# A third weight buffer for the experts of a transformer block, with x2 kept in memory meanwhile

## What is computed

```python
p_group = softmax(t @ w_rg + b_rg)          # 4 groups, the best one is taken
p_exp   = softmax(logits of its 4 experts)  # the best two are taken
y = sum over the two: weight * (silu(t @ w_gate[e]) * (t @ w_up[e])) @ w_down[e]
x = x2 + g2 * y
return rms_norm(x, final_norm)
```

## Time and profile before

| | us |
|---|---|
| median of 3 runs | 833.36 (833.19 to 833.53) |
| the profiled execution, whole | 836.89 |
| its span in the profile | 835.2 |
| routing ends, first gather issued | 507.03 |
| PE's last down product ends | about 800.5 |

### The profile page before, as it was taken

One profiled execution on the slowest core, in us unless ns is written; L12 is line 12 of the kernel. 1 busy time (PEld: TensorE's weight loads), 2 busy tenths in 40 slices (PEclk: granted clock), 3 DMA queues, 4 the chain that ended last, 5 costly groups with the idle time before them and its releaser, 6 DMA issues.

```text
span 835.2 us, 8861 instructions
## 1 busy us (share of the span) xinstructions
PE 702.7 (84%) x3377; PEld 397.4 (48%) x3377; DVE 335.3 (40%) x743; ACT 177.6 (21%) x427; POOL 131.2 (16%) x171
## 2 busy tenths in 40 slices
PE   0469899999999998889999815999998999899920
PEld 0455445667675796555544513444443344334300
DVE  4932566866575434867221174011211111021107
ACT  3203225121121213557121201111211112011103
POOL 8650022313050281000000001000000000000021
PEclk9669999999999998989999855999999999999975
DMA  9899802222220305510520422489999999999935
GB/s 335 262 312 276 288 0 101 101 102 101 101 101 1 53 1 192 191 73 2 202 94 19 168 97 64 165 281 401 374 388 396 381 399 383 399 369 397 398 110 230
DMA packets 88092, 173.49 MB, mean 208 GB/s; under 512 B 19347, under 2 KB 23533, under 8 KB 88045
## 3 DMA queue, kind: packets, MB, share of 16 engines
q1 hardware_dynamic: 78048, 151.12, 50.8%
q0 software_dynamic: 4240, 15.21, 5.6%
q10 hardware_dynamic: 5756, 6.52, 2.3%
HBM read 157.63 MB, written 15.20 MB: 207 GB/s over the span
## 4 chain that ended last, share of the span: by engine, by line
PE 66%; DVE 14%; DMA 12%; ACT 3%; issue 2%; POOL 1%; SPq 0%; ACTq 0%; POOLq 0%; DVEq 0%
PE ps L962 14%; DMA gu<-in_w_up 10%; PE ps L1067 7%; PE ps L2107 6%; PE ps L2074 5%; PE ps L955 3%; PE ps L989 3%; DVE acc L1733 3%; PE ps L2185 2%; PE ps L2191 2%; PE ps L2071 2%; PE ps L983 2%; PE ps L2098 2%; PE ps L2195 2%; PE ps L636 1%
## 5 line engine op out<-in xcount | busy, mean ns | idle before, releaser
L962 PE MATMUL ps<-gu,xgT 128*128 128x512 f32 x256 | 117.0, 617 | 8.3 <-DMA gu<-in_w_up 5.9
L962 PEld LDWEIGHTS ps<-gu,xgT 128*128 128x128 f32 x256 | 49.9, 198 | 70.5 <-issue 63.7
L1401 POOL DMA_INDIRECT xg<-xn_rows,list x16 | 15.0, 940 | 413.1 <-PE ps L943 221.2
L2107 PE MATMUL ps<-hT,winr 128*128 128x512 f32 x144 | 72.1, 609 | 0.0
L1733 DVE SCALAR_TENSOR_TENSOR acc<-ada,st,acc 128x512 f32<-128x512 f32 x84 | 68.1, 811 | 2.3
L1067 PE MATMUL ps<-wout,yT 128*128 128x512 f32 x128 | 58.6, 617 | 0.0
L955 PE MATMUL ps<-gu,xgT 128*64 128x512 f32 x256 | 56.7, 595 | 0.0
L989 PE MATMUL ps<-dn,hidT 128*128 128x512 f32 x128 | 56.5, 594 | 0.0
L1038 DVE TENSOR_TENSOR hidm<-sg,ps 128x512 f32<-128x512 f32 x8 | 5.5, 686 | 121.6 <-ACT sg L1005 121.6
L1587 POOL TENSOR_TENSOR cc<-low,lev 128x512 f32<-128x512 f32 x20 | 30.2, 1520 | 129.7 <-DVE low L1919 104.2
L2074 PE MATMUL ps<-hT,wind 128*128 128x512 f32 x96 | 42.3, 593 | 0.0
(11 more groups left out here) (401 smaller groups left out, 1041.9 us busy)
## 6 DMA issues: line engine op xcount, KB each, us to landing
gu<-in_w_gate SPq DMA_DIRECT2D x16, 2048.0 KB, 14.6
gu<-in_w_up SPq DMA_DIRECT2D x16, 2048.0 KB, 20.5
dn<-in_w_down SPq DMA_DIRECT2D x16, 2048.0 KB, 20.5
ada<-in_w_ada SPq DMA_DIRECT2D x12, 2048.0 KB, 10.4
expert_rows<-zero POOLq DMA_DIRECT2D x9, 512.0 KB, 10.8
expert_rows<-yo ACTq DMA_DIRECT2D x8, 512.0 KB, 6.7
wout<-in_w_out SPq DMA_DIRECT2D x1, 3072.0 KB, 10.7
x<-in_x SPq DMA_DIRECT2D x2, 1024.0 KB, 6.2
```

What stands on the lines that cost most here:

```text
L962: ins = nc.tensor.matmul(PS[2 * b + w][:, :], T["xgT"][:, k, :], gu[b][:, w, k, :], start=(k == 0), stop=(k == KT - 1))
L2107: ins = t.matmul(bank[:, :], w(k), T["hT"][:, k, :], start=(k == 0), stop=(k == KT - 1))
```

## The change

- A third buffer: `gu2` (32 KB a partition, from `RX`) and `dn2` (16 KB, in x2's place). Tile n uses buffer n % 3. SP issues gate/up n when gate/up n-3 is done and down n-1 when down n-4 is done.
- Experts 0, 1 and 2 are pinned. The order becomes B B B s B s B s B s B s B s s s; the tile sizes are the same, eight of 128 rows and eight of 64.
- x2 goes to memory in four stores behind the last `xn2` store, and comes back as `x3` (in the second down buffer's place) when down 13 is done. The final sum works on `x3`. `fnb` is loaded just before, after gate/up 14.
- Gate/up and down weights of expert 2 are loaded after the x2 stores are issued and after their room is free.
- g2 is copied out of `g2b` by ACT (`g2m`, `g2s`, and an unused `g2q`), before the routing's exponentials; DVE's two copies go.
- Routing: one link more in the tile starts, one operation more for the padded rank; `EXTRA` is 10. Several semaphores become one with counts (`routing`), set at the same places.

```diff
     at("x2", R1 + 64 * K + 256, [P, ST, D])
+    at("dn2", R1 + 64 * K + 256, [P, FT, D])
+    at("x3", RW + 16 * K, [P, ST, D])
...
+    at("gu2", RX, [P, 2, KT, F])
...
-    ORDER = [0, 1]
-    for m in range(BIG - 2):
-        ORDER += [BIG + m, 2 + m]
-    ORDER += [E - 2, E - 1]
+    ORDER = list(range(NBUF))
+    big, less = list(range(NBUF, BIG)), list(range(BIG, E))
+    rest = less[::-1] if NBUF == 3 else less
+    while big:
+        ORDER.append(rest.pop(0))
+        ORDER.append(big.pop(0))
+    ORDER += rest[::-1] if NBUF == 3 else rest
...
-        sp.dma_start(T["fnb"][:], A["final_norm"].partition_broadcast(P)).then_inc(sem("fn_in"), 16)
-        sp.wait_ge(sem("experts"), 1)
+        for i in range(ST):
+            sp.dma_start(x2_d[i * P:(i + 1) * P, :], T["x2"][:, i, :]).then_inc(sem("x2_st"), 16)
+        sp.wait_ge(sem("g2_moved"), 1)
+        sp.wait_ge(sem("ss"), 2 * ST)
+        sp.wait_ge(sem("logit_mm"), ST)
+        for b in range(2):
+            sp.wait_ge(sem(f"xn2_st{b}"), 32)
+        load_gate_up(sp, 2, 2)
+        sp.wait_ge(sem("x2_st"), 16 * ST)
+        load_down(sp, 2, 2)
+        sp.wait_ge(sem("routing"), ROUTING["experts"])
         expert = {}
-        for n in range(2, E + 1):
+        for n in range(NBUF, E + 1):
...
-                sp.wait_ge(sem("gu_mm"), n - 1)
-                load_gate_up(sp, expert[n], n % 2)
-            if n >= 3:
-                sp.wait_ge(sem("dn_mm"), n - 2)
-                load_down(sp, expert[n - 1], (n - 1) % 2)
+                sp.wait_ge(sem("gu_mm"), n - NBUF + 1)
+                load_gate_up(sp, expert[n], n % NBUF)
+            if n > NBUF:
+                sp.wait_ge(sem("dn_mm"), n - NBUF)
+                load_down(sp, expert[n - 1], (n - 1) % NBUF)
+
+        sp.wait_ge(sem("gu_mm"), E - 1)
+        sp.dma_start(T["fnb"][:], A["final_norm"].partition_broadcast(P)).then_inc(sem("fn_in"), 16)
+        sp.wait_ge(sem("dn_mm"), E - 2)
+        sp.dma_start(T["x3"][:], x2_d.rearrange("(i p) d -> p i d", p=P)).then_inc(sem("x3_in"), 16)
...
+        act.wait_ge(sem("oproj_mm"), ST)
+        act.wait_ge(sem("ada_out"), HPS - 4)
+        for name, m in (("g2m", P), ("g2s", 64), ("g2q", 32)):
+            d = D * m // P
+            for s in range(P // m):
+                ins = a.activation(T[name][m * s:m * s + m, :], T["g2b"][m * s:m * s + m, s * d:(s + 1) * d], ACT.Copy)
+        ins.then_inc(sem("g2_moved"), 1)
         act.wait_ge(sem("exp_in"), 1)
...
-        link(v.scalar_tensor_tensor(e16[:], rank, float(HALF), pad.unsqueeze(1).broadcast_to([P, ST, E]), ALU.is_ge,
-                                    ALU.mult))
+        wide_pad = pad.unsqueeze(1).broadcast_to([P, ST, E])
+        link(v.tensor_tensor(e16[:], rank, wide_pad, ALU.add))
+        link(v.scalar_tensor_tensor(e16[:], e16[:], float(P), wide_pad, ALU.is_ge, ALU.mult))
...
-        for e in range(2):
-            link(g.memset(T["pinned"][:, e:e + 1], (2 - e) * 1e6))
+        for e in range(NBUF):
+            link(g.memset(T["pinned"][:, e:e + 1], (NBUF - e) * 1e5))
```

More of the change, by code:

```diff
@@ L48 @@
 FT = F // P
[L49 to L53, removed]
+EXTRA = 10
+NBUF = 3
+ROUTING = {"chosen": 1, "places": 2, "slots": 3, "list": 4, "experts": 5, "w12": 6, "route_i": 7}
+ROUTING_PE = {"rank_mm": 1, "list_mm": 2}
+SIZES = [128] * 8 + [64] * 8
+TILE_START = [sum(SIZES[:n]) for n in range(E + 1)]
+TILE_START += [TILE_START[E] + P * (n + 1) for n in range(EXTRA - 1)]
 ROWS = TILE_START[-1] + P
+BIG = SIZES.count(P)
+STEPS_DOWN = [n for n in range(1, E) if SIZES[n] < SIZES[n - 1]]
 EPS = 1e-6
@@ L854, in build, with rows_of @@
     wd_v = A["w_down"][0].rearrange("g e (k p) d -> (g e) p k d", p=P)
-    gu, dn = (T["gu0"], T["gu1"]), (T["dn0"], T["dn1"])
-    ORDER = [0, 1]
-    for m in range(BIG - 2):
-        ORDER += [BIG + m, 2 + m]
-    ORDER += [E - 2, E - 1]
+    gu, dn = [T[f"gu{b}"] for b in range(NBUF)], [T[f"dn{b}"] for b in range(NBUF)]
+    ORDER = list(range(NBUF))
[5 more added lines that the diff above has]
+    ORDER += rest[::-1] if NBUF == 3 else rest
+    def rows_of(n):
+        return SIZES[ORDER[n]] if n < E else P
     def small(n):
-        return n < E and ORDER[n] >= BIG
-    NB = E // 2
+        return rows_of(n) < P
     STORED = [1]
     for n in range(E + EXTRA):
-        STORED.append(STORED[-1] + (2 if small(n) else 1))
+        STORED.append(STORED[-1] + P // rows_of(n))
     def load_gate_up(q, e, b):
@@ L940, in pe_rows @@
             pe.wait_ge(sem("xgT_d"), n)
-        m = HALF if small(n) else P
+        m = rows_of(n)
         for k in range(KT):
@@ L945, in pe_rows, with buffer_of, loads_of, pe_gate_up @@
         ins.then_inc(sem("xg_tr"), 1)
-    def pe_gate_up(pe, n, b, came):
-        pe.wait_ge(sem(f"gu_in{b}"), came)
+    def buffer_of(n):
+        return n % NBUF if n < E else 0
+    def loads_of(n):
+        if n < E:
+            return n // NBUF + 1
+        return len(range(0, E, NBUF)) + n - E + 1
+    def pe_gate_up(pe, n, b):
+        w_in = gu[buffer_of(n)]
+        pe.wait_ge(sem(f"gu_in{buffer_of(n)}"), 32 * loads_of(n))
         pe.wait_ge(sem("xgT_a"), n + 1)
         pe.wait_ge(sem("xgT_d"), n + 1)
+        m = rows_of(n)
         if small(n):
+            parts = P // m
+            f = F // parts
             for k in range(KT):
-                for s in range(2):
+                for s in range(parts):
                     ins = nc.tensor.matmul(
-                        PS[2 * b][HALF * s:HALF * s + HALF, :].rearrange("p (w f) -> p w f", w=2),
-                        T["xgT"][:, k, 0:HALF], gu[b][:, :, k, s * GW:(s + 1) * GW], start=(k == 0),
-                        stop=(k == KT - 1))
+                        PS[2 * b][m * s:m * s + m, 0:2 * f].rearrange("p (w f) -> p w f", w=2),
+                        T["xgT"][:, k, 0:m], w_in[:, :, k, s * f:(s + 1) * f], start=(k == 0), stop=(k == KT - 1))
         else:
@@ L968, in pe_hidden, with pe_down @@
         pe.wait_ge(sem("hidm"), n + 1)
-        for f in range(2 if small(n) else FT):
+        for f in range(FT * rows_of(n) // P):
             ins = nc.tensor.transpose(PS[2 * b][:, f * P:(f + 1) * P], T["hidm"][:, f * P:(f + 1) * P], idf[:])
         ins.then_inc(sem("hid_tr"), 1)
-    def pe_down(pe, n, b, came):
+    def pe_down(pe, n):
+        w_in = dn[buffer_of(n)]
         pe.wait_ge(sem("hidT"), n + 1)
-        pe.wait_ge(sem(f"dn_in{b}"), came)
+        pe.wait_ge(sem(f"dn_in{buffer_of(n)}"), 16 * loads_of(n))
         pe.wait_ge(sem("yo_d"), n + 1)
+        m = rows_of(n)
         if small(n):
+            parts = P // m
+            per = FT // parts
+            d = D // parts
             for f in range(FT):
[L981 to L985, removed]
+                s, c = f // per, f % per
+                for w in range(parts):
+                    ins = nc.tensor.matmul(PS[4][m * w:m * w + m, 0:d], T["hidT"][:, c, m * s:m * s + m],
+                                           w_in[:, f, w * d:(w + 1) * d], start=(f == 0), stop=(f == FT - 1))
         else:
@@ L1016, in act_output @@
         start = TILE_START[ORDER[n] if n < E else n]
[L1017 to L1023, removed]
+        m = rows_of(n)
+        d = D * m // P
+        for s in range(P // m):
+            act.dma_start(yo_d[start:start + m, s * d:(s + 1) * d], T["yo"][m * s:m * s + m, 0:d]
+                          ).then_inc(sem("yo_st"), 16)
     def dve_rows(dve, n):
         dve.wait_ge(sem("xg_tr"), n + 1)
-        m = HALF if small(n) else P
+        m = rows_of(n)
         for k in range(4, KT):
@@ L1128, in pe_moe @@
                            start=False, stop=(i == ST))
-        ins.then_inc(sem("rank_mm"), 1)
-        pe.wait_ge(sem("places"), 1)
+        ins.then_inc(sem("routing_pe"), 1)
+        pe.wait_ge(sem("routing"), ROUTING["places"])
         for n in range(2):
@@ L1282, in dve_moe @@
         link(v.tensor_reduce(order, versus, AX.X, ALU.add))
-        link(v.tensor_scalar(t16, order, -float(BIG), 0.0, ALU.add, ALU.max))
         link(v.tensor_scalar(tile0, order, float(P), None, ALU.mult))
-        v.scalar_tensor_tensor(tile0, t16, -float(P - HALF), tile0, ALU.mult, ALU.add)
-        link(v.tensor_scalar(pad, order, BIG - 0.5, float(P - HALF), ALU.is_gt, ALU.mult))
+        for m, n in enumerate(STEPS_DOWN):
+            less = float(SIZES[n - 1] - SIZES[n])
+            link(v.tensor_scalar(t16, order, -float(n), 0.0, ALU.add, ALU.max))
+            link(v.scalar_tensor_tensor(tile0, t16, -less, tile0, ALU.mult, ALU.add))
+            if m:
+                link(v.tensor_scalar(t16, order, n - 0.5, less, ALU.is_gt, ALU.mult))
+                link(v.tensor_tensor(pad, pad, t16, ALU.add))
+            else:
+                link(v.tensor_scalar(pad, order, n - 0.5, less, ALU.is_gt, ALU.mult))
         link(v.tensor_tensor(cnt, cnt, pad, ALU.add))
@@ L1321, in dve_moe @@
                                       T["tok"][:, i:i + 1], ALU.is_equal, ALU.mult)
[L1322 to L1325, removed]
```

(12 more changed lines are left out.)

69 lines of the change are left out of this document (37 added, 32 removed).

## The result

The changed kernel takes **825.07 us** (median of 5 runs, 824.21 to 829.30); the kernel before takes 833.36. The ratio is 0.9891, 95% interval 0.9862 to 0.9920: 1.1% faster; the medians differ by 8.3 us. The profiled execution took 829.30 with a span of 827.6, 7.6 us less than the span before.

A forecast was written before the change was run, and what follows sets the result against it. The prediction took the experts' stage to be bound by DMA at the margin, through short lead as much as rate. Terms -10.37 + 0.37 + 0.26 = -9.7 us took 833.36 to 823.7 us, range 821.5 to 829.

The forecast's parts named there:

- Starvation of 10.37 us goes: Experts' stage: PE's waits for gate/up weights and the slower products behind them vanish, 10.37 us gained.
- The early load in the idle stretch, done by 505: Before the experts: expert 2's weights load while DMA idles, ending about 505, ahead of the first gather at 507.03.
- The term of 0: First gather: collision with the early load was worth 0 to 2.1 us, and 0 was taken.
- the second rival: First gathers: the early load collides and gather 0 lands 2.1 us late, at most some 4; 825.8 to 828, chance 0.12.
- The lead of 41.8 us against 31 to 34: Big tiles' gate/up loads: a third buffer gives 41.8 us of lead instead of 19.9; landing needs 31 to 34 at worst.
- At the end, 28 us for a load of 10.6 with a backlog of about 10: Three last small tiles: gate/up 15 has 28 us before PE wants it, for a 10.6 us load plus backlog.
- PE should not wait at all: Experts' stage: PE never waits for weights, and its clock stays at 1.00 from the second product on.
- The added steps: DVE's routing chain gains 0.37 us, POOL's tenth empty `If` 0.26; ACT's g2 copies and x3's return cost nothing.
- Rival 1: Experts' stage: DMA's own pace stays the bound, PE waits some 5 us near the end; 828 to 829, chance 0.12.
- The rule: Experts' stage: at the skill's 358 GB/s an estimated 9 us would come back, giving about 832.8; the trace's 397 disagreed.

The follow-up runs named there:

- e3: The changed kernel with x2 stored four times instead of once, so expert 2's early loads run across the first gathers: 827.84 us, ratio 0.9919.
- e1: The changed kernel with expert 2's weights asked for only when gate/up 0 is done, so nothing streams during the routing: 834.01 us, ratio 0.9989.
- e9: The changed kernel with 2 MB copied memory to memory on SP's queue ahead of the load of gate/up 12: 831.62 us, ratio 0.9942.
- e6: The changed kernel with the four least chosen experts in tiles of 32 rows instead of 64, room for 12 extra tiles: 824.53 us, ratio 0.9864.
- e2: The changed kernel with gate/up n issued only when n-2 is done and down n-1 when n-3 is done, early load kept: 842.94 us, ratio 1.0098.
- e7: The changed kernel with 32-row tiles for four experts, hidden 15 copied ahead of store 14, and output 15 in its own tile: 822.14 us, ratio 0.9844.
- e5: The changed kernel with the old rank operation, no link in the tile starts and `EXTRA` = 9: 826.64 us, ratio 0.9886.
- r1: The changed kernel unaltered, run again in a second set of runs: 826.12 us against 836.90 before the change, ratio 0.9887.

## Why the prediction was right

The forecast was 823.7 us, the result 825.07. Its terms:

- *Starvation of 10.37 us goes.* Measured on the stage: 10.40. The step from the pairs' starts to this term was exact, the wait for gate/up is gone in all profiles of the change, and the clock with it: from the second on the big products take 13.7 to 14.0 us, none 15.71.
- *The early load in the idle stretch, done by 505.* It lay in the idle stretch, but its last part landed at 507.8, 3 us later than forecast. No wait of SP's did that, since DMA was at a share of 1.00 or more from 476 to 505; this profile's issues began 0.9 us later than those of the earlier trace rows, the last 15 us went at 391 GB/s instead of 397, and the rest isn't separated. The first gather, issued 1.6 us later than before, missed it by 0.8 us and landed in 4.58 us. The term of 0 was right with less margin than the sum gave. e3 shows the second rival with its forecast price of 2 to 4 us.
- *The lead of 41.8 us against 31 to 34.* Right where it was worked out: gate/up 9 ended at 687.47 (the big product of 695.58 follows it by 8.1 us), and the big product that needed the load began at 729.25. The load landed at 718.8, after 31.3 us; the forecast was 31 to 34.
- *At the end, 28 us for a load of 10.6 with a backlog of about 10.* This is the mis-sized term, and that PE didn't wait here is partly luck. By that sum 7.4 us were to spare; 1.7 us were. The second halves of the last four gate/up loads in the change, from SP's issues, the landing times and PE's chain (us):

| gate/up | issued | to landing | landed | product begins | spare |
|---|---|---|---|---|---|
| 12 | 690.81 | 28.0 | 718.8 | 729.25 | 10.4 |
| 13 | 711.08 | 26.7 | 737.8 | 747.80 | 10.0 |
| 14 | 730.24 | 25.2 | 755.4 | 762.74 | 7.3 |
| 15 | 748.45 | 24.2 | 772.65 | 774.34 | 1.7 |

Up to gate/up 12 the backlog was as forecast: when gate/up 12 ended, at 742.99, gate/up 14 needed another 12.4 us to land (10 to 13 forecast). But the sum for the end left out three terms that the prediction had counted for a big tile: the down load ahead (5.3), stores and gathers (3.5), start and receipt (2). With them it gives 31.4 us, and the load landed 29.7 us after 742.99. The sum also left out 3.4 us on PE's side, transposes for the most part: the product began 31.35 us after 742.99, not 28. The two omissions worked against each other, and the larger was DMA's. In the tail a load lands every 17.3 to 17.6 us, while PE's products begin 14.9 and then 11.6 us apart, so the spare falls from 10.0 to 1.7 us. "PE should not wait at all" came true by that 1.7. e1 and e9, with more bytes for DMA, and e6, with less work for PE, all bring the wait back.
- *The added steps.* Routing 0.40 (forecast 0.37), `If` 0.15 (0.26), ACT's copies and x3's return hidden, as costed. The copies, from ACT's timeline of the change, took 3.9 us, within the 3 to 7 forecast:

```profile
477.19 1.06 ACT L1228 ACTIVATE g2m<-g2b 128x1024 f32<-128x1024 f32 x1
478.14 1.26 ACT L1228 ACTIVATE g2s<-g2b 64x512 f32<-64x512 f32 x2
479.41 1.69 ACT L1228 ACTIVATE g2q<-g2b 32x256 f32<-32x256 f32 x4
```

- *Rival 1, the stream stays the bound*, got 0.12. It didn't come to pass in the time, but it describes what lies 2 us behind: remove the early load and PE waits 5.8 us late in the stage. (The prediction names slice 27 of the earlier trace rows as the first at 9 tenths; the row has 8 there and 9 from slice 28, which begins at the 564 us that it gives. Nothing hangs on it.)
- *The rule.* By an estimate from the figure of 358 GB/s in the Trainium skill, page "DMA: Bandwidth & Descriptors", section Specifications, almost nothing would have been gained. The trace has 387 and 389 GB/s at full share in the stage of the change. The Trainium skill, page "HBM Reference", section Specifications (TRN2), says that the two cores of a domain share its bandwidth and that one streaming alone measures well above its share. This kernel runs on one core, which fits; no run here shows two.

The medians differ by 8.3 us, and by 10.8 in the second set of runs, where the stage differs by 10.4. The added steps explain 0.5 of it. The rest lies within the scatter ahead of the routing and behind the experts that the table shows; nothing separates it further.

## What to carry to other kernels

When loads of fixed size feed an engine in turn, compare two things: the lead (from the free buffer to the first use) with the landing time at full streaming, and all bytes after the start with all the time until the last use. A further buffer mends the first, and only an idle stretch that it can fill mends the second; here, in one order of the tiles, each alone gave nothing or less. And look at the last load in the order: a tail of small tiles is where a stream that is slightly too slow collects its whole debt.

## What the runs showed that was not expected

- A shortage costs more than its gap: behind waits of 5.8 and 5.2 us for the last gate/up the product of 7.09 us took 8.57 and 10.02, at a mean granted clock of 0.82 and 0.70. Two runs with like gaps lost 1.5 and 2.9 us. For a big product a gap of 1.89 us in e2 cost 1.8 us more, and one of 1.97 us in e7 only 0.1 (clock 0.89 and 1.00). What decides between them was not tried.
- With `EXTRA` = 10 POOL issues the first gather 1.34 us after the list's conversion begins, in eight profiles; with 9 (before the change, and e5) and with 12 (e6, e7) after 1.01 to 1.04 us. The semaphores of e5 are those of the change, so these aren't it. What does it was not tried. The way from the logits to tile 0 is 51.66 us in r1 and in e5 all the same.
- The stage of the change repeats to 0.01 us (257.67, also in e5), while the part ahead of it scatters by 6.8 us over the profiles. A change within one stage is better measured there than in the time of the whole.
